# Where weight panels begin within 128 bytes, in a one-core transformer kernel: panels that move past standing activations at the activations' residue, in ring slots longer by 64 bytes

## The reference, cut to what matters

```python
for l in range(DEPTH):                       # block 1
    h = x @ w_in[l]                          # latents, q, k, v, gates
    # three branches: latent attention, differential attention, attention to mem
    merged = g0 * (o_mla @ wb0) + g1 * (o_diff @ wb1) + g2 * (o_mem @ wb2)
    x = layernorm(ALPHA * x + merged @ w_out[l])
    f = square(relu(x @ mlp_w1[l])) @ mlp_w2[l]
    x = layernorm(ALPHA * x + f)
for l in range(DEPTH):                       # block 2
    u = rmsnorm(h)
    # u @ w_in_2[l], three scans (hgrn, ssd, mlstm), gated branches, w_out_2
    h = h + merged @ w_out_2[l]
    up = dwconv(rmsnorm(h) @ w_up_2[l])      # 1024 -> 2 x 2816
    h = h + (silu(a) * v) @ w_down_2[l]
    h = h + (p[l] @ w_ple_2[l]) * sigmoid(h @ w_ple_gate_2[l])
return rmsnorm(h)
```

## Time and profile before

| | us |
|---|---|
| median of 3 runs | 2481.41 |
| lowest and highest run | 2479.23, 2483.37 |
| the profiled execution, its own time | 2486.97 |
| its span, first to last instruction | 2485.1 |
| mean granted TensorE clock over the span | 0.995 |

### The profile page before, as it was taken

One profiled execution on the slowest core, in us unless ns is written; L12 is line 12 of the kernel. 1 busy time (PEld: TensorE's weight loads), 2 busy tenths in 40 slices (PEclk: granted clock), 3 DMA queues, 4 the chain that ended last, 5 costly groups with the idle time before them and its releaser, 6 DMA issues.

```text
span 2485.1 us, 43110 instructions
## 1 busy us (share of the span) xinstructions
PE 2430.2 (98%) x17744; PEld 2225.9 (90%) x17744; DVE 1787.8 (72%) x2889; ACT 1451.0 (58%) x2130; POOL 287.6 (12%) x222
## 2 busy tenths in 40 slices
PE   8999999999999999899999999999999999999998
PEld 7888999888889899798999799998898999899996
DVE  4558675565586755589778897885599768887875
ACT  5547555545475555477656655664767656556654
POOL 0000002000000000002124710000012207500000
PEclk9999999999999999999999999999999999999999
DMA  7554476655545556554567646565554557645663
GB/s 246 160 141 125 154 253 192 203 181 167 141 119 153 185 189 204 166 159 123 154 189 200 198 134 194 184 190 190 145 159 137 172 173 205 181 151 186 190 209 127
DMA packets 358921, 430.50 MB, mean 173 GB/s; under 512 B 20617, under 2 KB 286311, under 8 KB 358469
## 3 DMA queue, kind: packets, MB, share of 16 engines
q1 hardware_dynamic: 341312, 401.72, 52.9%
q10 hardware_dynamic: 14340, 14.93, 2.7%
q0 software_dynamic: 3072, 11.10, 1.5%
HBM read 424.44 MB, written 3.24 MB: 172 GB/s over the span
## 4 chain that ended last, share of the span: by engine, by line
PE 86%; DVE 10%; ACT 2%; issue 1%; DMA 1%; ACTq 0%; POOL 0%; POOLq 0%; DVEq 0%
PE ps L112 84%; DVE wlo L121 3%; PE ps L115 2%; DVE sE L121 1%; DVE hgA L148 1%; DVE hgQF L121 0%; ACT L118 0%; DVE hgQB L121 0%; ACT lnv L118 0%; DVE hgkf L121 0%; DVE hgkb L121 0%; DMA kT<-in_diff_lambda 0%; DVE sbc L130 0%; DVE sE L124 0%; ACT whi L118 0%
## 5 line engine op out<-in xcount | busy, mean ns | idle before, releaser
L121 DVE TENSOR_TENSOR wlo<-wring,whi 128x1024 fp32r<-128x1024 f32 (+1 forms) x768 | 919.8, 1218 | 252.5 <-ACT whi L118 252.2
L118 ACT ACTIVATE whi<-wring 128x1024 fp32r<-128x1024 f32 (+1 forms) x768 | 803.4, 1054 | 428.3 <-PE ps L112 416.0
L112 PE MATMUL ps<-uT,whi 128*128 128x256 f32 x4640 | 821.7, 281 | 6.0 <-DVE wlo L121 4.7
L112 PEld LDWEIGHTS ps<-uT,whi 128*128 128x128 f32 x4640 | 706.4, 188 | 16.3 <-DVE wlo L121 8.1
L112 PE MATMUL ps<-uT,wlo 128*128 128x256 f32 x2320 | 646.8, 279 | 0.0
L112 PEld LDWEIGHTS ps<-uT,wlo 128*128 128x128 f32 x2320 | 437.5, 189 | 0.0
L112 PE MATMUL ps<-xT,whi 128*128 128x256 f32 x2112 | 375.0, 282 | 2.3 <-DVE xT L121 1.1
L112 PEld LDWEIGHTS ps<-xT,whi 128*128 128x128 f32 x2112 | 320.3, 187 | 9.4 <-issue 5.2
L112 PE MATMUL ps<-xT,wlo 128*128 128x256 f32 x1056 | 293.7, 278 | 0.0
L112 PE MATMUL ps<-whi,hid 128*128 128x512 f32 x864 | 269.5, 391 | 0.0
L112 PEld LDWEIGHTS ps<-xT,wlo 128*128 128x128 f32 x1056 | 197.8, 187 | 0.3
(11 more groups left out here) (400 smaller groups left out, 3565.4 us busy)
## 6 DMA issues: line engine op xcount, KB each, us to landing
wring<-in_w_in SPq DMA_DIRECT2D x346, 512.0 KB, 4.2
wring<-in_mlp_w SPq DMA_DIRECT2D x128, 512.0 KB, 4.5
wring<-in_w_up SPq DMA_DIRECT2D x88, 512.0 KB, 4.6
wring<-in_w_down SPq DMA_DIRECT2D x44, 512.0 KB, 4.3
wring<-in_w_branch SPq DMA_DIRECT2D x32, 512.0 KB, 3.4
wring<-in_w_out SPq DMA_DIRECT2D x32, 512.0 KB, 4.3
wring<-in_mem_w_kv SPq DMA_DIRECT2D x16, 512.0 KB, 6.4
wring<-in_w_br_hg SPq DMA_DIRECT2D x16, 512.0 KB, 4.7
```

Of the source, the lines that this page charges most:

```text
L112: return self.e.matmul(*p, **k) if self.e else Nothing()
L118: return self.e.activation(*p, **k) if self.e else Nothing()
L121: return self.e.tensor_tensor(*p, **k) if self.e else Nothing()
```

## The change

`half(b)` gives 1 for a buffer at residue 64 and 0 for one at residue 0. `panel` takes it as an argument. A slot of `whi` and `wlo` is now WS = 1040 elements long (4160 bytes), and its panel begins 0 or 16 elements into it, so that it lies at residue 0 for `half` 0 and at residue 64 for `half` 1. Only `projA` passes `half(x)`; `projB` and `narrow` leave 0. `wring` stays as it was. The two rings grow by 256 bytes each; to make room the constants shrink by 128 columns (512 bytes): the ones are now also the last piece of U, so they have moved between U and L. All activations keep their addresses. The ones are no longer in the first transfer; they are a transfer of their own at the end of `load_second`, with a wait in `latent_norm`, and the masks, left and right of them, are two transfers in place of one.

```diff
-C_ID, C_ONE, C_U, C_L, C_NU, C_NL, C_M, C_INV, C_EPS, C_END = (
-    0, 128, 256, 640, 1024, 1152, 1280, 2176, 2200, 2208)
+C_ID, C_U, C_ONE, C_L, C_NU, C_NL, C_M, C_INV, C_EPS, C_END = (
+    0, 128, 384, 512, 896, 1024, 1152, 2048, 2072, 2080)
...
-    t[:, C_U + 256:C_U + 384] = 1.0
...
+    def half(self, b):
+
+        return (self.base // 4 + b.off) // 16 % 2
+
...
-NW, WN, NS, LEAD = 5, 1024, 4, 3
+NW, WN, WS, NS, LEAD = 5, 1024, 1040, 4, 3
...
-    K.whi, K.wlo = sb("whi", NS * WN, F32R), sb("wlo", NS * WN, F32R)
+    K.whi, K.wlo = sb("whi", NS * WS, F32R), sb("wlo", NS * WS, F32R)
...
-    def panel(parts, nk, nb):
+    def panel(parts, nk, nb, half=0):
...
-        w, s = (i % NW) * WN, (i % NS) * WN
+        w, s = (i % NW) * WN, (i % NS) * WS
+        s += 16 * ((s // 16 + half) % 2)
...
-                p = panel([(0, w[...])], nk, nb)
+                p = panel([(0, w[...])], nk, nb, ar.half(x))
...
     def latent_norm(c, u):
         bank_free(u)
+        e.wait_ge(*at("ones"))
...
         e.dma_start(cst[:, C_INV:C_END], a["consts"][:, C_INV:C_END]).then_inc(*up("consts", "consts", by=16))
+        e.dma_start(K.ones, a["consts"][:, C_ONE:C_L]).then_inc(*up("ones", "ones", by=16))
...
-        e.dma_start(K.cst[:, C_U:C_INV], a["consts"][:, C_U:C_INV]).then_inc(*up("masks", "masks", by=16))
+        e.dma_start(K.cst[:, C_U:C_ONE], a["consts"][:, C_U:C_ONE]).then_inc(*up("masks", by=16))
+        e.dma_start(K.cst[:, C_L:C_INV], a["consts"][:, C_L:C_INV]).then_inc(*up("masks", "masks", by=16))
```

More of the change, by code:

```diff
@@ L447, in projA @@
                 nk = min(step, chunks - k0)
-                p = panel([(0, w[r0 + k0 * 128:r0 + (k0 + nk) * 128, c0 + b0:c0 + b0 + nb])], nk, nb)
+                p = panel([(0, w[r0 + k0 * 128:r0 + (k0 + nk) * 128, c0 + b0:c0 + b0 + nb])], nk, nb, ar.half(x))
                 do("tokens", p, x, us, k0_ + k0, first and k0 == 0, fin and k0 + nk == chunks)
```

## The result

| | before | after |
|---|---|---|
| median, us | 2481.41 of 5 runs | 2490.76 of 5 runs |
| lowest and highest run | 2477.79, 2483.37 | 2489.32, 2491.50 |
| the profiled execution, its span | 2486.97, 2485.1 | 2489.32, 2487.5 |

The ratio after to before is 1.0036, with the interval [1.0025, 1.0047]. The kernel is 9.3 us slower, beyond the top of the predicted range (2483.5).

What follows compares the result with a forecast made beforehand. The prediction took TensorE, busy 98% of the span, as the bound; 2.9 + 0.7 + 0.2 = 3.8 us off the 2481.4 us median gave 2477.6 us, with a range of 2472.5 to 2483.5.

Steps and rivals of the forecast that it cites:

- item 4: Longer ring slots change addresses only; standing panels stay at residue 0, and ScalarE and VectorE accesses cost nothing.
- Items 1 and 2: Panels moving past activations: 110 whole ones from 228.9 to 226.7 ns win 2.9 us; nine at 233.4 win 0.7 us.
- Item 3: Some 76 panels broken by transposes or score matmuls, above all xT's: nothing counted, at most 2.0 us won.
- Items 5 to 7: Constants: smaller first transfer wins 0.2 us at the start; ones issued later, new wait and split masks transfer cost nothing.
- the forecast's own range: Range if all goes as summed, 2475.5 to 2479.5 us, chance 0.45.
- Slower than before: Rival: pairs at 64 and 64 always meet at 233.4 ns, 110 whole panels lose 5.9 us; 2487.1; chance 0.07.
- Slower feature panels behind equal pairs: Rival: in block 1's MLPs, three handovers of 8 standing panels turn slow, 2.6 us lost; 2480.2; chance 0.14.
- A long stretch turns quick: Rival: layer 0's up projection in block 2 goes from 117.8 to 113.3 ns, 4.5 us more won; 2473.1; chance 0.22.
- Nothing changes: Rival: the standing operand's residue alone sets the pace; only the start's 0.2 us stays; 2481.2; chance 0.12.

Runs made afterwards that it cites:

- micro: Kernel of matmuls alone, none of the reference: nine panel-to-activation distances, 0 to 256 bytes; 226.7 to 234.4 ns with 512 moving columns, 113.3 to 120.0 with 256.
- v256: Changed kernel with slots of 4352 bytes, placed modulo 256: panels moving past activations at distance 0, standing panels at +64; 2482.93 us, ratio 1.0008 to before.
- micro2: Matmuls alone: panels at constant or alternating distances, unbroken or with four transposes behind each; alternating tokens 230.7 ns unbroken, broken features 38.1 to 39.9 us per 12 panels.
- before_4: The kernel before, unchanged, run and profiled again; 2480.98 us, span 2479.2.
- const_only: Changed kernel with slots of 1024, no panel placing and every buffer where it was before, keeping only the constants' new order, transfers and wait; 2481.23 us, ratio 0.9999.
- micro3: Matmuls alone: four tokens panels at five placings, then eight features panels at +64; features at 117.8 or 113.3 ns, eight entries per placing.
- v256_last: v256 with the last panel of each projection with standing activations left 64 bytes past them; median of 12 runs 2480.67 us, ratio 0.9994 to before.

## Why the prediction was wrong

**The step that failed** is item 4, "Slots of 1040: ring addresses only", with the bookkeeping under it, which counted residues modulo 128 as the change itself does. Two pairs that this makes equal can be 128 bytes apart modulo 256, and the measured pace there is 232.5, not 226.7. The trace of before couldn't contradict the count, since in it every slot was at 128 modulo 256; the arithmetic 4160 = 16 x 256 + 64 was there to be done, though no row of it said that 256 mattered. What the runs showed in its place: the longer slots alone, with no panel placed by its activations, take 2489.21 us where before took 2481.49 in the same session (slots_only), 7.7 us for a term that was put at nothing.

**Items 1 and 2** (won 2.9 + 0.7 us). In place of 2.22 ns won, 110 panels lost 1.5 ns a matmul (228.9 to 230.4): 110 x 12 x 1.5 = 2.0 us lost. The 76 panels that already had distance 0, which the prediction left out as untouched, went from 226.7 to 230.4. Some 68 of them are whole: 68 x 12 x 3.7 = 3.0 us lost. The nine at 233.4 did go, by 9 x 12 x 3.0 = 0.3 us. That is 4.7 us lost; the profiles show 5.5 (16.0 to 21.5), in both of after. The rest is in the 85 panels that were broken, 0.9 us more, 0.010 us each. The two starting paces were read rightly, and so was the cause behind them: micro has 228.9 at 64 and 226.7 at 0 with nothing else different. v256 has the sum of items 1 and 2: tokens 2.8 us below before, for the 3.6 of the forecast.

**Item 3** (nothing). Right to within the 0.9 us above, which micro2 has too (3.21 us for 3.20 per panel). The chain's broken pieces of xT come out at 2.79 us where the earlier trace rows has 2.76. The chain of after:

```profile
69.86 2.79 PE ps L111 x12
72.65 0.44 PE ps L114 x4
73.08 2.79 PE ps L111 x12
```

**Panels that stand.** The prediction had them stay at one residue. Half of them are now at 192. Against before_4, whose time is nearest to the median of before, the span of after is 8.3 us longer: tokens 5.9, the rest of features 4.0, whole features panels 2.2 less, and 0.6 elsewhere. micro2 suggests where the 4.0 may come from, since alternating distances cost 0.042 us per broken panel there: 95 such panels would do it, and about 150 of after's run at neither 113.3 nor 117.8. The profiles don't confirm it. Matched panel by panel, the features panels that are broken in both kernels (119 and 115) lose 1.7 us against before_4 and 4.8 against before. So some 5.5 to 6 of the 9.3 us are tokens, and that is shown. That the remainder is features is argued: in the mean of the five profiles of before, features stand at 48.9 us, in the mean of the two of after at 48.0. How the loss splits in the median run stays open.

**Items 5 to 7.** mem's transfer takes 5.48 and 5.40 us in after, 5.38 in const_only and 5.03 in slots_only, against 5.44 to 5.80 in the five profiles of before. The 0.2 us may well be there; const_only's ratio can't show it. The moved ones, the new wait and the extra issues cost nothing that can be measured (const_only, 0.9999 [0.9990, 1.0008]), as forecast. The top of the forecast's own range, 2479.5, comes from none of its items: their bounds give 2475.3 to 2477.8.

**The rivals.** *Slower than before* had the right sign and nearly the price (2487.1), but another mechanism: it wanted 64 against 64 to meet always, and in v256, where the pairs are equal, tokens run at 226.7. *Slower feature panels behind equal pairs* is a true mechanism, shown by v256, micro3 and v256_last, yet not what made this change slow. It is at work in after, where each w1 stretch behind w2 has its first four or five panels at 117.8. But against before_4, 48 whole panels in all went from 113.3 to 117.8 (4.9 us lost) and 63 the other way (6.4 us won), so that after has fewer whole panels at 117.8 than before. *A long stretch turns quick* describes scatter between executions and not an effect of a change; one profile of a bistable stretch doesn't tell which kernel it belongs to. *Nothing changes* (the standing residue alone sets the pace) is refuted by micro, where the standing activations stay put and the panel alone moves: 226.7 to 234.5 ns.

## What to carry to other kernels

Before an operand's address is changed, sweep the distance of the two operands once in a kernel of matmuls alone, over a range wider than the modulus that the change speaks of (micro takes 0.65 ms and gave the period). Then list where every tensor and every slot of a ring begins, with the modulus that the sweep shows, and for each kind of use (moving past, standing under) separately; a slot length that is no multiple of that modulus gives a pattern over the slots, and a mean over a stretch hides it. Where a gain of 0.1% is at stake, profile the unchanged kernel several times first, since stretches here fell into one of two paces, differently in each execution of the same program, worth more than the gain. A stretch made quicker can hand a slower pace to its neighbour, so time both.

## What the runs showed that I had not expected

- Matmuls of fp32r run at a pace that depends on the distance of the two operands' start addresses, with a period of 256 bytes: 226.7 to 234.5 ns for 512 moving columns, 113.3 to 120.0 ns for 256. At distance 0 the first kind is at its best and the second at its worst (120.0, as at 160). The Trainium skill, "SBUF — State Buffer", section "SBUF: two separate sides", has TensorE's reads never wait on anyone. The runs show only that a pair of TensorE's own operands costs up to 6% in its pace by where they begin; what inside the chip does it, no run shows.
- At +64 there are two steady paces (113.3 and 117.8; 228.9 and 233.4), and what ran just ahead bears on the choice: behind 0, 0, 0, 64 features take the quick one in 8 of 8, behind 0, 0, 0, 0 the slow one in 8 of 8, behind 64 throughout 5 to 3.
- Standing panels that are slow at a constant 192 (117.8 in 6 of 6) come down to 113.3 where 192 alternates with 64, at once or behind three panels. The slots of the kernel after make the same pattern, and both its profiles have fewer whole panels at 117.8 (95 and 97) than any of the five of before (116 to 195).
- Four of the five profiled executions of the kernel before (2486 to 2491 us) lie above nearly all its timed runs (median 2481.4), while those of after don't. Whether profiling favours the slow pace wasn't tried.
